# A hybrid attention and retention layer: gate and retention-query jobs ahead of the output jobs in every unit, all call lists redrawn

## The reference

```python
h = rms_norm(x, norm_gain)
aq, ak, av, ag, rq, rk, rv, rg = jnp.split(h @ w_in, SPLIT_POINTS, axis=-1)
attn = window_attention(aq, ak, av, q_norm_gain, k_norm_gain, sink_logits)
ret = retention(rq, rk, rv, ret_norm_gain)
mixed = jnp.concatenate([attn * jax.nn.silu(ag), ret * jax.nn.silu(rg)], axis=-1)
x = x + mixed @ w_out
```

## Time and profile before

| | us |
|---|---|
| median of 3 executions (1569.06 to 1569.93) | 1569.11 |
| the profiled execution | 1569.28 |
| its span, first to last instruction | 1567.47 |
| PE busy | 1555.1 |
| DVE busy | 1109.5 |
| ACT busy | 835.6 |
| POOL busy | 379.1 |

### The profile page before, as it was taken

One profiled execution on the slowest core, in us unless ns is written; L12 is line 12 of the kernel. 1 busy time (PEld: TensorE's weight loads), 2 busy tenths in 40 slices (PEclk: granted clock), 3 DMA queues, 4 the chain that ended last, 5 costly groups with the idle time before them and its releaser, 6 DMA issues.

```text
span 1567.5 us, 24792 instructions
## 1 busy us (share of the span) xinstructions
PE 1555.1 (99%) x8132; PEld 1358.3 (87%) x8132; DVE 1109.5 (71%) x2899; ACT 835.6 (53%) x2332; POOL 379.1 (24%) x365
## 2 busy tenths in 40 slices
...
GB/s 314 318 292 306 168 322 233 246 202 231 283 250 220 136 191 179 152 247 122 204 216 196 247 151 175 220 85 247 183 150 276 147 203 191 140 189 134 172 214 54
DMA packets 122639, 321.56 MB, mean 205 GB/s; under 512 B 17680, under 2 KB 59024, under 8 KB 122512
## 3 DMA queue, kind: packets, MB, share of 16 engines
...
## 4 chain that ended last, share of the span: by engine, by line
PE 92%; DVE 3%; ACT 1%; DMA 1%; issue 1%; SPq 1%; POOL 0%; ACTq 0%; DVEq 0%; POOLq 0%
PE jb L1408 26%; PE jb L1410 26%; PE jb L1409 26%; PE s L1443 2%; PE ob L1467 2%; PE ptb L1452 2%; PE ob L1427 1%; PE s L1506 1%; PE ab L1517 1%; PE s L1505 1%; DMA stage<-wp_dram 1%; PE s L1344 1%; SPq L362 0%; PE s L1346 0%; PE s L1507 0%
## 5 line engine op out<-in xcount | busy, mean ns | idle before, releaser
L1408 PE MATMUL jb<-wH,hTH 128*128 128x512 f32 (+1 forms) x1024 | 375.2, 366 | 5.7 <-DVE hTL L1146 4.5
L1410 PE MATMUL jb<-wH,hTL 128*128 128x512 f32 (+1 forms) x1024 | 372.0, 363 | 0.0
L1409 PE MATMUL jb<-wL,hTH 128*128 128x512 f32 (+1 forms) x1024 | 371.9, 363 | 0.0
L1408 PEld LDWEIGHTS jb<-wH,hTH 128*128 128x128 f32 x1024 | 193.2, 189 | 24.8 <-DVE wL L862 4.9
L1410 PEld LDWEIGHTS jb<-wH,hTL 128*128 128x128 f32 x1024 | 192.9, 188 | 20.5
L1409 PEld LDWEIGHTS jb<-wL,hTH 128*128 128x128 f32 x1024 | 193.2, 189 | 17.8
L1408 PE MATMUL jb<-wH,mxH 128*128 128x512 f32 x512 | 206.5, 403 | 0.0
L1408 PE MATMUL jb<-hTH,wH 128*128 128x512 f32 x512 | 201.0, 393 | 0.0
L1410 PE MATMUL jb<-wH,mxL 128*128 128x512 f32 x512 | 200.6, 392 | 0.0
L1409 PE MATMUL jb<-wL,mxH 128*128 128x512 f32 x512 | 200.3, 391 | 0.0
L1410 PE MATMUL jb<-hTH,wL 128*128 128x512 f32 x512 | 199.7, 390 | 0.0
...
## 6 DMA issues: line engine op xcount, KB each, us to landing
wH<-scrH SPq DMA_DIRECT2D x144, 512.0 KB, 7.3
wL<-scrL SPq DMA_DIRECT2D x144, 512.0 KB, 7.9
stage<-wp_dram SPq DMA_DIRECT2D x48, 512.0 KB, 6.7
scrH<-wH SPq DMA_DIRECT2D x48, 512.0 KB, 6.6
scrL<-wL SPq DMA_DIRECT2D x48, 512.0 KB, 7.3
...
xt<-xT_dram SPq DMA_DIRECT2D x15, 512.0 KB, 6.8
```

The source lines that it names most:

```text
L1408: pe.matmul(o, lh, rh_, start=i == 0, stop=False)
L1409: pe.matmul(o, lh, rl_, start=False, stop=False)
L1410: m = pe.matmul(o, ll, rh_, start=False, stop=i == last)
```

## The change

The phases of a unit come in another order: G of unit n ahead of O of unit n - 1. All lists are drawn anew, by a list scheduler, to fit. The five small inputs (norm gain, retention gain, q and k gains, identity) come as one array laid out on the host, in one transfer, first of all. The warm-up has 18 matmuls in place of 12. On SP each save is issued as soon as its turn allows it, panel (n,1) goes ahead of panel (n-1,3), the store of a finished block behind panel (n,2), and the refill of the residual rows behind panel (n+1,0). The arithmetic is the same. The core of the diff:

```diff
-        return [("Q", n), ("O", n - 1), ("G", n), ("V", n)]
+        return [("Q", n), ("G", n), ("O", n - 1), ("V", n)]
...
-WARM = 12
+WARM = 18
+SMALL = KT + RET_HEADS + 2 + P
...
-        rgain = sb("rgain", [P, RET_HEADS])
-        ident = sb("ident", [P, P])
-        ngain = sb("ngain", [P, KT])
-        qkg = sb("qkg", [P, 2])
+        small = sb("small", [P, SMALL])
+        ngain, rgain, qkg, ident = small[:, 0:8], small[:, 8:16], small[:, 16:18], small[:, 18:SMALL]
...
+            saved = [5]
+
+            def save_to(end):
+
+                for i in range(saved[0], end):
+                    low_of(sp, 2 * i)
+                    low_of(sp, 2 * i + 1)
+                    save(i)
+                saved[0] = max(saved[0], end)
...
-                    if q >= STAGES:
-                        save(q - STAGES)
+                    save_to(q - STAGES + 1)
...
+                if old in SPLIT_AT:
+                    save_to(4 * SPLIT_AT[old] + 4)
...
-            sp.dma_start(ngain[:, :], norm_gain.rearrange("(k p) -> p k", p=P), allow_slow_non_contiguous=True
-                         ).then_inc(S["s_gains"], 16)
+            sp.dma_start(small[:, :], small_in).then_inc(S["s_gains"], 16)
...
-            sp.dma_start(ident[:, :], c_ident).then_inc(S["s_ident"], 16)
...
-            sp.dma_start(rgain[:, :], ret_gain.rearrange("(k p) -> p k", p=P), allow_slow_non_contiguous=True
-                         ).then_inc(S["s_rgain"], 16)
-            for half in range(2):
-                rows = slice(half * HD, half * HD + HD)
-                sp.dma_start(qkg[rows, 0:1], q_gain.rearrange("(d o) -> d o", o=1)).then_inc(S["s_qkg"], 16)
-                sp.dma_start(qkg[rows, 1:2], k_gain.rearrange("(d o) -> d o", o=1)).then_inc(S["s_qkg"], 16)
...
                 attention_constants(n)
+                panel(n, 1)
                 panel(n - 1, 3)
...
-                panel(n, 1)
                 retention_constants(n)
+                panel(n, 2)
                 if u == 0:
                     store(b - 1)
-                panel(n, 2)
+                panel(n + 1, 0)
                 if u == 0:
                     refill(b)
-                panel(n + 1, 0)
```

Of the new lists, the parts that the prediction speaks of. POOL's start:

```diff
+            xpow(0, 0); rpow(0, 0); xpow(0, 1); wl1(0, 1, 0); wl1(0, 1, 1); wl1(0, 1, 2); xpow(0, 2); wl1(0, 1, 3)
+            wl1(0, 1, 4); xpow(0, 3); wl1(0, 1, 5); rpow(0, 1); rpow(0, 2); wl1(0, 1, 6); wl1(0, 1, 7); rpow(0, 3)
```

DVE in unit 4, in unit 8, and where unit 9 goes over into unit 10:

```diff
+            qk_norm(4, 3); mtl(3, 3); tql(4, 2); part1(4, 2); tql(4, 3); agz(4, 0); wl1(3, 3, 7); carry_out(4)
...
+            ptl(8, 0); carry_out(8); part2(8, 1); part1(8, 2); agz(8, 0); agz(8, 1); part1(8, 3); agg(8, 0)
...
+            gnm(9, 2); rupd(9, 3); v_parts(10, 0); qk_stats(10, 0); gna(9, 3); gnb(9, 2); rl(10, 0); qk_norm(10, 0)
+            mtl(9, 1); gnv(9, 3); gnm(9, 3); qk_stats(10, 1); v_parts(10, 1); tql(10, 0); qk_norm(10, 1); gnb(9, 3)
```

ACT at the same three places:

```diff
+            mth(3, 3); tqh(4, 2); xrb_copy(1); tqh(4, 3); exps(4, 2); ag(4, 0); obcopy(4, 0); pth(4, 1); ag(4, 1)
...
+            v_shift(8, 3); mth(7, 3); tqh(8, 3); pth(8, 0); exps(8, 1); xrb_copy(2); pth(8, 1); obcopy(8, 0)
...
+            rh(9, 3); ocopy(9, 2); mth(9, 0); qkv(10, 0); ocopy(9, 3); gnx(9, 2); rh(10, 0); v_shift(10, 0); mth(9, 1)
```

PE at the start, in unit 4, in unit 8 and from unit 9 to 10 (unit 12 is as unit 8):

```diff
+            job(0, 0); job(0, 1); job(0, 2); TQ(0, 0); job(0, 3); XB(0); S_(0, 0); job(0, 4); TQ(0, 1); job(0, 5)
...
+            I(3, 2); MT(3, 0); job(4, 1); I(3, 3); MT(3, 1); TQ(4, 0); job(4, 2); TQ(4, 1); S_(4, 0); MT(3, 2)
+            job(4, 3); S_(4, 1); job(4, 4); PT(4, 0); job(4, 5); MT(3, 3); TQ(4, 2); S_(4, 2); TQ(4, 3); XB(1)
+            job(4, 6); PT(4, 1); S_(4, 3); PV(4, 0); job(4, 7); PT(4, 2); job(3, 12); PV(4, 1); job(3, 13); job(3, 14)
...
+            MT(7, 3); TQ(8, 3); S_(8, 1); PT(8, 0); job(8, 6); S_(8, 2); PT(8, 1); XB(2); PV(8, 0); S_(8, 3)
+            job(8, 7); PT(8, 2); job(7, 12); PV(8, 1); job(7, 13); job(7, 14); PT(8, 3); A(8, 0); job(7, 15); A(8, 1)
...
+            A(9, 3); I(9, 1); job(9, 11); I(9, 2); MT(9, 0); job(10, 0); I(9, 3); MT(9, 1); job(10, 1); MT(9, 2)
+            TQ(10, 0); job(10, 2); TQ(10, 1); S_(10, 0); MT(9, 3); job(10, 3); S_(10, 1); job(10, 4); TQ(10, 2)
```

More of the change, by code:

```diff
@@ L276, in panel @@
                     if (n, p) == SPLITS[-1]:
[L277 to L280, removed]
+                        save_to(4 * len(SPLITS))
                 else:
@@ L465, in _ @@
[L465 to L469, removed]
@@ L485, in _ @@
[L485 to L489, removed]
@@ L490, in _ @@
[L490 to L498, removed]
-            mixl(13, 3); gpow(13, 1); rpow(14, 0); gpow(13, 2); rpow(14, 1); rpow(14, 2); gpow(13, 3); rpow(14, 3)
@@ L847, in _ @@
-            mth(15, 1); ocopy(15, 3); obcopy(15, 2); pth(15, 3); gnx(15, 3); mixh(15, 2); obcopy(15, 3); mth(15, 2)
-            mixh(15, 3); mth(15, 3)
+            rh(0, 0); wh1(0, 0, 0); wh1(0, 0, 1); wh1(0, 0, 2); wh1(0, 0, 3); xh(0, 0, 0); wh1(0, 0, 4); wh1(0, 0, 5)
+            xh(0, 0, 1); wh1(0, 0, 6); wh1(0, 0, 7); xh(0, 0, 2); xh(0, 0, 3); xsq(0, 0); xh(0, 1, 0); xh(0, 1, 1)
+            xh(0, 2, 0); qkv(0, 0); xsq(0, 1); xh(0, 2, 1); wh1(0, 1, 0); wh1(0, 1, 1); v_shift(0, 0); xh(0, 3, 0)
@@ new lines, in _ @@
+            wh1(1, 1, 6); wh1(1, 1, 7); rh(1, 0); ocopy(0, 3); gnx(0, 2); mth(0, 1); v_shift(1, 1); qkv(1, 2)
+            gnx(0, 3); v_shift(1, 2); wh1(0, 3, 0); wh1(0, 3, 1); wh1(0, 3, 2); wh1(0, 3, 3); tqh(1, 0); mth(0, 2)
+            qkv(1, 3); wh1(0, 3, 4); wh1(0, 3, 5); v_shift(1, 3); tqh(1, 1); mth(0, 3); ag(1, 0); wh1(0, 3, 6)
+            wh1(0, 3, 7); exps(1, 0); xsq(1, 0); ag(1, 1); xsq(1, 1); tqh(1, 2); rqh(1); pth(1, 0); exps(1, 1)
+            wh1(1, 2, 0); wh1(1, 2, 1); wh1(1, 2, 2); wh1(1, 2, 3); wh1(1, 2, 4); wh1(1, 2, 5); tqh(1, 3); exps(1, 2)
@@ new lines, in _ @@
+            wh1(2, 1, 2); wh1(2, 1, 3); wh1(2, 1, 4); wh1(2, 1, 5); ocopy(1, 2); mth(1, 0); qkv(2, 0); wh1(2, 1, 6)
+            wh1(2, 1, 7); v_shift(2, 0); qkv(2, 1); gnx(1, 2); rh(2, 0); ocopy(1, 3); v_shift(2, 1); mth(1, 1)
+            qkv(2, 2); tqh(2, 0); v_shift(2, 2); gnx(1, 3); mth(1, 2); wh1(1, 3, 0); wh1(1, 3, 1); wh1(1, 3, 2)
+            wh1(1, 3, 3); wh1(1, 3, 4); wh1(1, 3, 5); tqh(2, 1); exps(2, 0); mth(1, 3); qkv(2, 3); tqh(2, 2)
+            wh1(1, 3, 6); wh1(1, 3, 7); v_shift(2, 3); ag(2, 0); xsq(1, 2); tqh(2, 3); ag(2, 1); xsq(1, 3); exps(2, 1)
@@ new lines, in _ @@
+            kwh_ah(2, 2); ocopy(2, 1); rh(2, 2); gnx(2, 1); rvg(2, 3); wh1(3, 1, 0); wh1(3, 1, 1); mth(2, 0); rh(2, 3)
+            wh1(3, 1, 2); kwh_ah(2, 3); wh1(3, 1, 3); wh1(3, 1, 4); wh1(3, 1, 5); ocopy(2, 2); qkv(3, 0); wh1(3, 1, 6)
+            wh1(3, 1, 7); v_shift(3, 0); qkv(3, 1); mth(2, 1); gnx(2, 2); rh(3, 0); ocopy(2, 3); v_shift(3, 1)
+            qkv(3, 2); tqh(3, 0); v_shift(3, 2); gnx(2, 3); mth(2, 2); wh1(2, 3, 0); wh1(2, 3, 1); wh1(2, 3, 2)
+            tqh(3, 1); wh1(2, 3, 3); wh1(2, 3, 4); wh1(2, 3, 5); mth(2, 3); qkv(3, 3); exps(3, 0); tqh(3, 2)
@@ new lines, in _ @@
+            rvg(3, 2); xh(1, 2, 0); xh(1, 2, 1); gnx(3, 0); xh(1, 3, 0); xh(1, 3, 1); rvg(3, 3); kwh_ah(3, 2)
+            ocopy(3, 1); rh(3, 2); qkv(4, 0); kwh_ah(3, 3); rh(3, 3); ocopy(3, 2); mth(3, 0); v_shift(4, 0); gnx(3, 1)
+            qkv(4, 1); ocopy(3, 3); tqh(4, 0); gnx(3, 2); v_shift(4, 1); mth(3, 1); qkv(4, 2); tqh(4, 1); mth(3, 2)
+            exps(4, 0); rh(4, 0); wh1(3, 3, 0); v_shift(4, 2); wh1(3, 3, 1); wh1(3, 3, 2); wh1(3, 3, 3); wh1(3, 3, 4)
+            qkv(4, 3); wh1(3, 3, 5); gnx(3, 3); exps(4, 1); pth(4, 0); v_shift(4, 3); wh1(3, 3, 6); wh1(3, 3, 7)
@@ new lines, in _ @@
+            tqh(7, 3); exps(7, 2); rqh(7); pth(7, 1); exps(7, 3); obcopy(7, 0); rk(7); pth(7, 2); obcopy(7, 1)
+            kwh_ah(7, 0); mixh(7, 0); pth(7, 3); obcopy(7, 2); mixh(7, 1); obcopy(7, 3); mixh(7, 2); rvg(7, 0)
+            xh(2, 0, 0); xh(2, 0, 1); rqz(7); xh(2, 1, 0); rvg(7, 1); kwh_ah(7, 1); ocopy(7, 0); xh(2, 1, 1); rh(7, 1)
+            rvg(7, 2); xh(2, 2, 0); xh(2, 2, 1); mixh(7, 3); gnx(7, 0); xh(2, 3, 0); rvg(7, 3); kwh_ah(7, 2)
+            ocopy(7, 1); rh(7, 2); mth(7, 0); qkv(8, 0); xh(2, 3, 1); v_shift(8, 0); gnx(7, 1); qkv(8, 1)
@@ new lines, in _ @@
+            mth(11, 2); tqh(12, 2); rh(12, 0); gnx(11, 3); exps(12, 0); v_shift(12, 3); mth(11, 3); tqh(12, 3)
+            pth(12, 0); exps(12, 1); xrb_copy(3); pth(12, 1); obcopy(12, 0); exps(12, 2); ag(12, 0); ag(12, 1); rk(12)
+            exps(12, 3); rqh(12); pth(12, 2); obcopy(12, 1); mixh(12, 0); rqz(12); kwh_ah(12, 0); mixh(12, 1)
+            pth(12, 3); obcopy(12, 2); obcopy(12, 3); mixh(12, 2); mixh(12, 3); rvg(12, 0); rvg(12, 1); kwh_ah(12, 1)
+            rh(12, 1); ocopy(12, 0); gnx(12, 0); rvg(12, 2); ocopy(12, 1); kwh_ah(12, 2); rh(12, 2); rvg(12, 3)
@@ new lines, in _ @@
+            gnx(12, 1); kwh_ah(12, 3); ocopy(12, 2); rh(12, 3); mth(12, 0); qkv(13, 0); ocopy(12, 3); gnx(12, 2)
+            rh(13, 0); v_shift(13, 0); mth(12, 1); qkv(13, 1); tqh(13, 0); v_shift(13, 1); gnx(12, 3); mth(12, 2)
```

(6 more changed lines are left out.)

821 lines of the change are left out of this document (394 added, 427 removed).

## The result

The changed kernel took **1616.96 us** (median of 3 executions, 1616.26 to 1620.77), against 1569.11 before: a ratio of 1.0312, 95% interval 1.0297 to 1.0326. That is 47.9 us slower. The prediction was 1575.5, in a range of 1564 to 1581: right in sign, far too small, and outside its range.

A forecast was written before the change was run, and what follows sets the result against it. It took TensorE, busy nearly the whole span, as the bound. From the profiled 1569.28, -1.5 + 2.95 + 3.6 + 1.5 = +6.55, less 0.17, gave 1575.7, stated as 1575.5 us; range 1564 to 1581.

The forecast's parts named there:

- unit 4: S_(4,2) waits for the chain TQ, tqh, tql with no PE work between: 2.95 us, no clock loss taken.
- units 8 and 12: S_(n,3) waits 0.45 us for part1, job(n,7) 1.3 for agz: 1.8 us each, 3.6 together.
- The other units: PE comes close behind its suppliers, as at MT(9,2): 1.5 us for all, between 0 and 6.
- one chain, through ACT: MT(9,2) wants ab, freed by mtl(9,1): about 4.3 us from I(9,3) against PE's 0.14 + 4.2, within 0.3 either side.
- The start: First 172 us: most of the early win given to a new wait, -1.5 us, between -6.95 and +2.
- Its parts: Earlier first job 1.5 us, high clock 2.3, job(0,3) stall 1.15, small pieces 2.0: 6.95 gained, against POOL's new wait.
- The wait foreseen for XB(0): Block 0: XB(0) ahead of job(0,4) waits some 2 us for POOL's last xpow, done at 30.9 us.
- the first rival: Block-start waits absorbed and start won, if the last xpow ends before 29 us: 1562 to 1565, chance 0.20.
- Block starts: Units 4, 8 and 12: adjacent producer and consumer in PE's list expose whole chains, 2.95 + 3.6 us.
- Transfers: SP's new order of panels, store and refill costs nothing, as each panel lands during the Q phase.
- The rivals: Waits absorbed, start won: 1562 to 1565, 0.20; halves cancel: 1566 to 1572, 0.25; unit 4 clock drop: 1578 to 1581, 0.15.

The follow-up runs named there:

- after_fills: The changed kernel with all 216 GpSimd subtractions turned into fills of the same tiles, lists untouched: 1592.5 us.
- relist_lock_fills: The changed kernel with 135 calls moved, placed with VectorE held up by GpSimd's subtractions, and all 216 subtractions turned into fills: 1574.5 us.
- mtl_sooner: The changed kernel with mtl(n,1) moved ahead of rl(n+1,0) and qk_norm(n+1,0) in VectorE's list, units 5, 9, 13 and 14 only: 1616.7 us.
- before_fills: The kernel before the change with GpSimd's subtractions turned into fills, as a control: 1566.5 us.
- relist_lock: The changed kernel with 135 calls moved, placed with VectorE held up by GpSimd's subtractions, which stay: 1582.4 us.

## Why the prediction failed

The loss by stretches, compared call by call, beside what the prediction put at each:

| stretch | put at | measured |
|---|---|---|
| start, up to job(1,0) | -1.5 | -1.5 |
| units 1 to 3, up to job(4,0) | in the 1.5 below | 17.5 |
| unit 4 | 2.95 | 5.7 |
| units 8 and 12 | 3.6 | 5.6 |
| units 5 to 7, 9 to 11, 13 to 15 | 1.5 for all other units | 18.1 |
| behind the last job | nothing | 1.5 |

**The failed step** is "The other units": "I take 1.5 us for all, between 0 and 6." They lose 35.6 us, half of it in units 1 to 3 and half behind unit 5, by two causes.

*Behind unit 5 it is the order of the lists.* The method was the flaw: I worked out one chain, through ACT, gave DVE 0.417 us for mtl, named rl(10,0) ahead of it without giving it a time, and did not count qk_norm(10,0); the trace shows them in the way with 0.58, 0.49 and 0.22 us. after_fills, which still loses 20 us from job(5,0) on, and relist_lock_fills, which loses 5 (1085.7 us from there to the last job, before 1080.8), show that this is the order; mtl_sooner shows why a wait counted singly is no measure of it.

*In units 1 to 3 it is the port*, which the prediction did not have. after_fills loses nothing there: it goes from 2.7 us ahead of before at job(1,0), call by call, to 3.6 ahead at job(4,0). That the cause is that DVE is held, and not that GpSimd is late, rests on after_fills, on DVE's waits for GpSimd and on the stretched rows. The trace of the kernel before could have told it: there too the maximum of mixr is three and a half times its median.

```profile
L1008 DVE TENSOR_TENSOR mixr<-rawqn,gate x128: 416/421/1507, 73.2 to 1538.4; 64x256 f32<-64x256 f32 x128
```

**The start** came out at the -1.5 us that it was put at, but not by the parts that it was added up from, so the size is luck.

**Its parts.** The first job did start sooner, at 8.82 us, without matmuls at 1.2 GHz, as foreseen; job(0,1) was 2.5 us ahead of before. The wait foreseen for XB(0), a sign by which the prediction called itself wrong, did not come: rpow ran at 17.47 us, not 20, and the last xpow ended just before PE came:

```profile
28.18 0.70 POOL L458 TENSOR_TENSOR xr<-xm,mhalf 128x2 f32<-128x2 f32 x1
```

```profile
28.98 0.60 PE L1527 MATMUL ab<-small,xr 128*128 128x128 f32 x4
```

By the first rival's test, xpow done before 29 us, the whole start would have been won. It was not: TQ(0,0) waited 0.93 us and S_(0,3) 2.12, which the prediction had not counted.

**Block starts** were the right places. Units 8 and 12: 1.1 us of waits each at the calls foreseen (S_(n,3) 0.14, job(n,7) 0.95) against 1.8, and 2.8 us lost in each unit in all; relist_lock_fills keeps both waits. Unit 4: S_(4,2) waited 3.42 us by the timeline, foreseen 2.95. But the clock did fall behind it, which I had left out of the sum; windows of PE after it (PEclk is the third figure from the end):

```profile
435.20:437.20 2.00, 2.00 (x12) 2.00 (x12) 1.15 (x2) 0.00 (x0) 0.00 (x0) 0.64 0.00 0
437.20:439.20 2.00, 2.00 (x7) 1.62 (x6) 1.25 (x4) 1.67 (x4) 0.00 (x0) 0.51 0.00 0
439.20:441.20 2.00, 2.00 (x10) 1.64 (x10) 1.82 (x4) 1.76 (x10) 0.00 (x0) 1.00 0.00 0
```

Unit 4 lost 5.7 us in all, call by call. The page on the clock gate of the Trainium skill, "TensorE: Matmul & The Clock Gate" (Why this matters for your kernels), cited in the prediction, would have had it so; here the trace agrees with it.

**Transfers**, put at nothing, made PE wait nowhere by its list of waits, but DVE waits 40.6 us for the sinks because its new list takes them in sooner. The prediction checked the panels alone.

**The rivals** were all drawn from the same few places, so none reached the case that came. Against before_fills (1566.5) the changed kernel is 50.5 us slower, by the medians: 24.5 for the port (to after_fills), 18.0 for the order of the lists with the port out of play (to relist_lock_fills), and 8.0 that remain. Call by call these 8.0 are: the start 1.4 shorter, unit 4 2.6 longer, units 8 and 12 1.8 and 1.6, everything else up to the last job 1.8, and 1.5 behind it. So with this one order of the lists the three block starts cost 6.0 us, where the prediction had said 6.55; whether another order would take these too was not run. The rest of the loss lay in the port and in how the lists were drawn. Order and port overlap: relist_lock took 34.6 us by order alone, the port still in play.
